# Delta rule of a four-mixer block: ScalarE forms the convolution's first tap, and the value tiles' convolutions and transposes stand among the inverse's levels

## What is computed

```
h = rmsnorm(x, n_pre_mix); proj = h @ w_in
qkv = silu(causal_dwconv(gdn_qkv, conv_w))          # 4 taps, 1536 channels
qa, ka, va = split(qkv)                             # 4 heads of 128 each
qa = l2norm(qa) * 128 ** -0.5; ka = l2norm(ka)
beta = sigmoid(gdn_b); g = -exp(a_log) * softplus(gdn_a + dt_bias)
# per chunk, with gc = cumsum(g):
lower = where(strict, (k_beta @ k.T) * decay, 0)
t_inv = inverse(eye + lower)                        # triangular
u, w = t_inv @ v_beta, t_inv @ (k_beta * exp(gc))
# scan over chunks: v_new = u - w @ state; o = q_dec @ state + attn @ v_new; state update
```

## Time and profile before

| | |
|---|---|
| median of 3 runs | 2614.05 us |
| profiled execution | 2617.91 us, span 2616.1 us |
| PE (matmuls) busy | 2432.9 us, 93% |
| POOL busy | 1329.2 us, 51% |
| DVE busy | 1003.9 us, 38% |
| ACT busy | 735.0 us, 28% |
| mean granted TensorE clock | 0.969 |

### The profile page before, as it was taken

One profiled execution on the slowest core, in us unless ns is written; L12 is line 12 of the kernel. 1 busy time (PEld: TensorE's weight loads), 2 busy tenths in 40 slices (PEclk: granted clock), 3 DMA queues, 4 the chain that ended last, 5 costly groups with the idle time before them and its releaser, 6 DMA issues. The chain is left out here.

```text
span 2616.1 us, 29905 instructions
## 1 busy us (share of the span) xinstructions
PE 2432.9 (93%) x11636; PEld 1989.6 (76%) x11636; DVE 1003.9 (38%) x1278; ACT 735.0 (28%) x1332; POOL 1329.2 (51%) x764
## 2 busy tenths in 40 slices
PE   7899998999998989999788899989999989899997
PEld 6688776777786768888677887767777867688885
DVE  4863314334444331122258633143345343311222
ACT  3334225222125121122133342252221251211221
POOL 4612552555642546677456026435555435466773
PEclk9999999999999999999989999999999999899998
DMA  4301221322220223322033003213222212232221
GB/s 154 89 17 33 86 77 47 105 81 81 58 84 29 97 81 97 96 98 97 26 99 89 17 33 89 81 41 113 81 81 56 80 35 97 81 97 97 97 97 49
DMA packets 109670, 198.76 MB, mean 76 GB/s; under 512 B 6608, under 2 KB 25040, under 8 KB 109136
## 3 DMA queue, kind: packets, MB, share of 16 engines
q1 hardware_dynamic: 108368, 190.45, 23.5%
q10 hardware_dynamic: 1152, 6.29, 0.7%
HBM read 194.62 MB, written 2.10 MB: 75 GB/s over the span
## 5 line engine op out<-in xcount | busy, mean ns | idle before, releaser
L490 POOL TENSOR_SCALAR ring_hi<-stage 128x1024 fp32r<-128x1024 f32 (+4 forms) x380 | 402.2, 1058 | 1218.7 <-PE big L1399 1165.4
L492 POOL TENSOR_TENSOR ring_lo<-stage,ring_hi 128x1024 fp32r<-128x1024 f32 (+4 forms) x380 | 928.2, 2443 | 31.7
L1399 PE MATMUL big<-h_hi,ring_hi 128*128 128x512 f32 x1712 | 677.9, 396 | 1.7 <-POOL ring_lo L492 1.0
L1399 PE MATMUL big<-h_lo,ring_hi 128*128 128x512 f32 x1712 | 667.0, 390 | 0.0
L1399 PE MATMUL big<-h_hi,ring_lo 128*128 128x512 f32 x1712 | 666.7, 389 | 0.0
L1399 PEld LDWEIGHTS big<-h_hi,ring_hi 128*128 128x128 f32 x1712 | 321.6, 188 | 73.4 <-issue 5.6
L1399 PEld LDWEIGHTS big<-h_lo,ring_hi 128*128 128x128 f32 x1712 | 321.4, 188 | 68.4
L1399 PEld LDWEIGHTS big<-h_hi,ring_lo 128*128 128x128 f32 x1712 | 321.8, 188 | 67.1 <-issue 2.9
L1399 PE MATMUL big<-ring_hi,h_hi 128*128 128x512 f32 (+2 forms) x896 | 345.3, 385 | 14.2 <-ACT scr L802 5.8
L1399 PE MATMUL big<-ring_lo,h_hi 128*128 128x512 f32 (+2 forms) x896 | 344.1, 384 | 0.0
L1399 PE MATMUL big<-ring_hi,h_lo 128*128 128x512 f32 (+2 forms) x896 | 344.1, 384 | 0.0
(11 more groups left out here) (236 smaller groups left out, 2555.7 us busy)
## 6 DMA issues: line engine op xcount, KB each, us to landing
stage<-in_w_in SPq DMA_DIRECT2D x160, 512.0 KB, 3.6
stage<-in_w_mlp_in SPq DMA_DIRECT2D x64, 512.0 KB, 3.8
stage<-in_w_mlp_out SPq DMA_DIRECT2D x64, 512.0 KB, 3.4
stage<-in_w_o SPq DMA_DIRECT2D x16, 512.0 KB, 3.4
stage<-in_w_br_a SPq DMA_DIRECT2D x8, 512.0 KB, 3.6
stage<-in_w_br_c SPq DMA_DIRECT2D x8, 512.0 KB, 3.5
stage<-in_w_br_d SPq DMA_DIRECT2D x8, 512.0 KB, 3.4
stage<-in_w_br_b SPq DMA_DIRECT2D x8, 512.0 KB, 3.4
```

Source lines behind the costliest of these rows:

```text
L490: nc.gpsimd.tensor_scalar(rH[jw][0:pp, r, 0:kk, 0:job.n], w, 1.0, 0.0, ALU.mult, ALU.add).then_inc(sem("w_hi"), 1)
L492: nc.gpsimd.tensor_tensor(rL[jw][0:pp, r, 0:kk, 0:job.n], w, f32(rH[jw][0:pp, r, 0:kk, 0:job.n]), ALU.subtract).then_inc(sem("w_ready"), 1)
L1399: ins_ = MM(o_, a_, r_, start=s0, stop=s1)
```

## The change

ACT forms the first tap of every convolution (`conv_base`, a Copy with the tap as scale into `g_cv`), DVE keeps the three `scalar_tensor_tensor`. For q, `conv_base(0)` and `(1)` stand after the four raw copies, the later ones behind the Silus; for k likewise. The bases of tiles 8 and 9 follow the small gate terms; Silus 8 and 9 with bases 10 and 11 follow the copies of `gatea0`; Silus 10 and 11 and the table load stand before ACT's work of level 3. DVE runs `conv(8)` before the cumulative sums' copy, `conv(9)` between `exponents(0)` and `lower(0)`, `conv(10)` and `(11)` at the head of levels 1 and 2. PE's `fill(1)` behind `gc` moves behind `scores_gdn(1)`, and `natural_k_v(0)` moves to the head of level 4, with its wait for the twelve Silus.

```diff
@@ mixer_keys
     for b0 in (0, 2):
-        k += [("T0", b0), ("T0", b0 + 1), ("kn", b0), ("vn", b0)]
+        k += [("T0", b0), ("T0", b0 + 1)]
+        k += [("kn", b0), ("vn", b0)] if b0 else []
         for n in range(1, LEVELS):
+            k += [("kn", 0), ("vn", 0)] if (b0, n) == (0, 4) else []
@@ ScalarE
+                def conv_base(i):
+                    big_freed(act, (("aq", "ak", "av")[i // 4], i % 4))
+                    if i >= 2:
+                        act.wait_ge(sem("a_silu"), i - 1)
+                    A(g_cv[:, i % 2, :], (aQ, aK, aV)[i // 4][:, i % 4, :], ACT.Copy, scale=lw[:, LCW + 36 + i:LCW + 37 + i]).then_inc(sem("a_base"), 1)
                 qkv_raw(0)
+                conv_base(0)
+                conv_base(1)
                 for i in range(4):
                     conv_silu(i)
                     if i < 2:
+                        conv_base(i + 2)
                         qk_squares(i)
...
                 qkv_raw(1)
+                conv_base(4)
+                conv_base(5)
                 for i in range(4, 8):
                     conv_silu(i)
                     if i < 6:
+                        conv_base(i + 2)
                         qk_squares(i)
...
-                for i in range(8, 12):
-                    conv_silu(i)
-                exp_ln_tables()
+                conv_base(8)
+                conv_base(9)
...
                 gate_copy("a", 0)
+                for i in (8, 9):
+                    conv_silu(i)
+                    conv_base(i + 2)
...
                     for n in range(1, LEVELS):
+                        if b0 == 0 and n == 3:
+                            conv_silu(10)
+                            conv_silu(11)
+                            exp_ln_tables()
@@ VectorE, conv(i)
-                    if i >= 2:
-                        dve.wait_ge(sem("a_silu"), i - 1)
+                    dve.wait_ge(sem("a_base"), i + 1)
-                    TS(cv, raw, tap(3), None, ALU.mult).then_inc(sem("a_tap"), 1)
...
-                for i in range(8, 12):
-                    conv(i)
+                conv(8)
...
-                for b in range(2):
-                    exponents(b)
-                    lower(b)
-                    scores_and_first_level(b)
+                exponents(0)
+                conv(9)
+                lower(0)
+                scores_and_first_level(0)
+                exponents(1)
+                lower(1)
+                scores_and_first_level(1)
                 for b0 in (0, 2):
-                    natural_k_v(b0)
+                    if b0:
+                        natural_k_v(b0)
                     for n in range(1, LEVELS):
+                        if b0 == 0 and n in (1, 2):
+                            conv(9 + n)
+                        if b0 == 0 and n == 4:
+                            natural_k_v(0)
@@ TensorE
                 done(MM(ps[:, 0:16], triu, s_g...), "gc")
-                fill(1)
                 pe.wait_ge(sem("a_l2"), 8)
...
                     scores_gdn(b)
-                pe.wait_ge(sem("a_silu"), 12)
+                fill(1)
                 for b0 in (0, 2):
...
-                    natural_k_v(b0)
+                    if b0:
+                        natural_k_v(b0)
                     for n in range(1, LEVELS):
+                        if b0 == 0 and n == 4:
+                            pe.wait_ge(sem("a_silu"), 12)
+                            natural_k_v(0)
```

More of the change, by code:

```diff
@@ L1029, in conv @@
                     big_freed(dve, key)
-                    if i >= 2:
-                        dve.wait_ge(sem("a_silu"), i - 1)
+                    dve.wait_ge(sem("a_base"), i + 1)
                     cv, raw = g_cv[:, i % 2, :], (aQ, aK, aV)[i // 4][:, i % 4, :]
                     tap = lambda q: lw[:, LCW + 12 * q + i:LCW + 12 * q + i + 1]
-                    TS(cv, raw, tap(3), None, ALU.mult).then_inc(sem("a_tap"), 1)
                     for q in (1, 2):
-                        dve.wait_ge(sem("a_tap"), 3 * i + q)
                         STT(cv[:, q:], raw[:, 0:S - q], tap(3 - q), cv[:, q:], ALU.mult, ALU.add).then_inc(sem("a_tap"), 1)
-                    dve.wait_ge(sem("a_tap"), 3 * i + 3)
+                        dve.wait_ge(sem("a_tap"), 2 * i + q)
                     STT(cv[:, 3:], raw[:, 0:S - 3], tap(0), cv[:, 3:], ALU.mult, ALU.add).then_inc(sem("a_conv"), 1)
```

## The result

The changed kernel takes 2629.6 us (median of 4 runs, 2626.38 to 2633.11) against 2614.97 us (4 runs, 2612.47 to 2617.98). The ratio is 1.0051, 95% interval 1.0039 to 1.0063: slower by 10 to 16 us. The forecast was 2627.5 us and slower.

A forecast was written before the change was run, and what follows sets the result against it. PE, busy 93% of the span, was taken as the bound. Per layer, +7.7 for k tiles, -3.85 or -6.7 from gates to first Y, +4.3 in levels: +13.45 on 2614.05 gives 2627.5 us, range 2608 to 2636.

The forecast's parts named there:

- What bounds the kernel: Whole kernel: PE is busy 93% of the span, so only its waits or low clock can change the time.
- Part 1: k convolutions: they start behind four raw copies, conv(7) ends 5.4 us late, PE waits for the Ln; 7.7 us per layer.
- low clock: PE's granted clock drops behind its waits; taken as 2.3 us behind the Ln, 1.6 at lower(1), 1.6 in level 1.
- the start: k convolutions: conv(4) starts near 66.5 instead of 61.84, with 12 instructions left, 3 more than before at that point.
- the count of places: k convolutions: one DVE instruction ends per POOL instruction; one place fewer makes the wait 3.9 us, one more 8.2.
- Rival A: k convolutions: without DVE's tensor_scalar, DVE and POOL run free and conv(7) ends before 81.7; 2603.9 us, chance 0.12.
- Part 2: Gates to first Y: PE needs 39.4 us per layer, gaining 3.85 us in layer 0 and 6.7 in layer 1.
- The table load: ACT's Silu and Exp/Ln table switches: 1.28 us each, leaving out the skill page's 1.38 us drain.
- Part 3: Inverse levels: low clock 1.6 us in level 1, X of level 3 1.8 late, kn and vn 0.9; 4.3 per layer.
- The sum: Both layers: +8.15 us in layer 0 and +5.3 in layer 1, together +13.45.
- Rival B: New waits don't lower the clock and L1102 slips in before POOL: no change, 2611.5 us, chance 0.17.

The follow-up runs named there:

- e3: The changed kernel with bases 0, 1, 4 and 5 put between the raw copies instead of behind all four; 2610.54 us, ratio 0.998.
- e4: The changed kernel with one of the three scalar_tensor_tensor left out in each of the four k tiles; 2611.02 us, ratio 0.9983.
- e1: The changed kernel with all four taps of q and k kept on DVE, leaving the value tiles' part alone; 2607.42 us, ratio 0.9975.
- e5: e3's kernel with Silus 8 and 9 and bases 10 and 11 ahead of the copies of gatea0; 2599.58 us, ratio 0.9944.
- e8: e3's kernel with DVE's three products for key_decays(1) ahead of chunk 0's masks; 2610.32 us, ratio 0.998.
- e9: The kernel with all four edits together, and exponents(1) on DVE moved ahead of chunk 0's masks; 2587.90 us, ratio 0.9899.
- e6: e3's kernel with Silu 10, Silu 11 and the table load each in another level, the Silus between Y and V copies; 2610.12 us, ratio 0.9974.
- all four edits together: The changed kernel with the edits of e3, e5, e6 and e8 combined; 2593.41 us, ratio 0.9916.

## Why the prediction was right, point by point

- **What bounds the kernel.** Right: the loss came at the one row with no slack, the Ln, and no other engine's busy time counted. DVE's fell from 1003.9 to 984.1 us while the kernel got slower.
- **Part 1, the late k tiles.** Right. `conv(7)` ends 5.2 us later by the span's clock and 6.1 by the layer's start (5.4 forecast), and PE waits 5.72 (layer 0) and 5.74 us where 5.6 was forecast. From the first sums of squares to the next ones PE needs 9.99 and 10.19 us where it needed 7.57 and 7.59, so the low clock cost 2.4 and 2.6 (2.3 forecast). Still the term was a little small, +8.6 and +8.2 against 7.7. What it left out lies ahead of the Ln: in both layers PE falls back 0.65 us where it takes weights from POOL's ring: it waits 0.74 us there and waited 0.48 before (below, first after, then before), and loses 0.4 more at the next unit. In layer 1 the first transposes took 0.6 us less and hid it.

```profile
72.22 0.50 PE L1424 MATMUL big<-h_hi,ring_hi 128*128 128x512 f32 x1 [0.74 <-POOL ring_lo L494]
```

```profile
72.95 0.50 PE L1399 MATMUL big<-h_hi,ring_hi 128*128 128x512 f32 x1 [0.48 <-POOL ring_lo L492]
```

  That it is the start (e3) and the count of places (e4, 2.1 us each) is shown. Rival A is out: with no `tensor_scalar` of DVE's left, two `scalar_tensor_tensor` still took 4.3 us beside POOL.
- **Part 2, the gain.** Right: from the end of `gates_by_token` to the first Y PE needs 39.3 us in both layers (39.4 forecast). The 6.92 us wait went; 2.51 us stood at `lower(1)` in both layers (2.5 forecast) and 4.48 us before the first Y (4.2). The low clock at `lower(1)` cost 1.6 us, as forecast: 9.0 us up to `T0` against 7.4 in e1. e5 shows the cause of the wait before the first Y. For the one at `lower(1)` the prediction named L1102 behind POOL. e8 shows that this alone was 0.9 of the 2.5 us: with it gone, the masks behind POOL hold `exponents(1)` for the other 1.6, which e9 removes.
- **The table load.** Leaving out a drain was right. The load takes 1.28 us and the next ACTIVATE starts 0.01 us after it, here as before:

```profile
141.14 0.60 ACT L539 ACTIVATE scr<-big 128x512 f32<-128x512 f32 x1 [0.76 <-PE big L1424]
141.76 1.28 ACT L578 ACT_TABLE_LOAD   x1
143.05 0.63 ACT L578 ACTIVATE scr<-scr 128x512 f32<-128x512 f32 x1
143.78 0.72 ACT L574 ACTIVATE scr<-scr,lw 128x512 f32<-128x512 f32 x1
```

  The Trainium skill, "ScalarE: Activation LUTs", section "What ACT_TABLE_LOAD costs", puts a drain of 1.38 us on each switch to another set. By it, as an estimate, the wait before the first Y would have been 5.6 us (the 4.2 forecast and 1.38); the trace differs, with 4.48 and no drain. The scaled Copy takes 0.72 us there, not the 0.64 taken from L524, where four stand back to back.
- **Part 3, the levels.** X of level 3 waits 1.54 and 1.55 us (1.8 forecast). Low clock behind the 4.48 us wait: 5.29 and 5.38 us for 32 matmuls that take 3.76 in the next level, so 1.5 and 1.6 (1.6 forecast). In all, the stretch from the first Y to the last V grew by 3.7 and 3.8 us where 4.3 was forecast.
- **The sum.** +13.45 forecast; +13.5 in the touched sections of the profiled executions, +14.6 between the medians. That the first two agree to 0.1 us is luck: part 1 came out 1.4 us larger than forecast, parts 2 and 3 together 1.35 smaller. The low clock was partly luck too. The prediction read its cost behind the 6.92 us wait, 3.0 us, from layer 0 alone; in layer 1 of the kernel before, 16 of the 32 matmuls behind the same wait took 3.61 us and the next 16 their normal 1.95, which is 1.6. Its terms of 1.6 held in this execution, while in layer 1 of e3, in both of e6 and in layer 0 of e8 the same 4.48 us wait cost some 4.4 instead of 1.5. Rival B, no low clock, is out by the 0.50 behind the wait.

## What to carry to other kernels

An instruction taken from an engine is worth its duration only if the engine was what others waited for and its start stays where it was; look first for the consumer with zero wait. Where the rows show two engines' instructions ending in turn, as DVE's and POOL's here, count places, not microseconds: an instruction of 0.77 us was worth 2.1 us (e4). For those of 0.49 us the nearest measure is e3 against before: with two of them fewer beside POOL, `conv(7)` ends 3.8 us earlier, though it starts 0.8 later. When work moves to another engine, place it by what that engine's list holds ahead of it (four raw copies, the copy that waits for the last filler, the Y copies); all three bad places here could be mended by moving a few lines (e3, e5, e6).

## What the runs showed that I had not expected

- The cost of one and the same wait. Behind 4.48 us of idle PE, the next 40 instructions took 6.0 us or 8.8 us, in two layers of one execution. Low clock can therefore hide what a wait was worth: e6 and e8 removed 3.1 and 1.9 us of waiting and gained 0.4 and 0.2, while all four edits together gained 17.1. In some traces the low clock came behind the next wait when one was gone (level 3 in e5, level 1 in layer 0 of e8). That the removed wait is the cause was not tried: in e6 the same stretch of level 1 got longer with nothing changed ahead of it.
- Low clock in untouched code: one execution of before and one of after differ by 4.1 us in the some 1150 us of layer 0 that no edit touches, in several places; the largest has PE fully busy at 0.83 in one and 1.00 in the other. The changed kernel's four runs fall in two pairs, 2626.4 and 2627.2, 2632.0 and 2633.1. That the pairs have this cause was not tried.
